# A two-part transformer kernel: token layout in the experts' stage, 512-wide scatter products, and a reordered end of three stages

## The reference

```python
for l in range(2):
    sh_m, sc_m, g_m, sh_f, sc_f, g_f = split(silu(c) @ ada_w[l] + ada_b[l], 6)
    h = rmsnorm(x, norm_mix[l]) * (1 + sc_m) + sh_m
    # three branches: differential attention, latent attention, state space (ssd)
    y = grouped_rmsnorm(ssd(...) * silu(z))          # 4 groups of 256 columns
    merged = sig(ga)*(ya@w_branch_a) + sig(gb)*(yb@w_branch_b) + sig(gc)*(y@w_branch_c)
    x = x + g_m * (merged @ w_out[l])
    h = rmsnorm(x, norm_ffn[l]) * (1 + sc_f) + sh_f
    x = x + g_f * (ffn(h @ ffn_w_up) @ ffn_w_down[l])
h = x + concat(oa, ob) @ w_out_2                      # attention of the second part
u = rms_norm(h, norm2_g)
# one group of 4, then 2 of its 8 experts per token; 32 experts of 1024 -> 512 -> 1024
y[token] += gate * (silu(u @ w_gate[e]) * (u @ w_up[e])) @ w_down[e]
out = rms_norm(h + y, final_norm_g)                   # (1, 256, 1024)
```

## Time and profile before

| | |
|---|---|
| median of 3 runs | 2047.88 us (2047.69 to 2048.53) |
| the profiled execution: its time, its span | 2048.76 us, 2047.0 us |
| busy: PE (matmul) / PEld (weight load) | 1930.3 us (94%) / 1380.8 us (67%) |
| busy: DVE (VectorE) / ACT (ScalarE) / POOL | 646.2 us (32%) / 411.3 us (20%) / 0.8 us |
| granted TensorE clock, mean | 0.967 of full speed |
| read from HBM | 439 MB, 215 GB/s over the span |

### The profile page before, as it was taken

How to read it: one execution, slowest core, us unless ns; L and a number is a source line. 1 busy time by engine, 2 the same in 40 slices (tenths; PEclk the granted TensorE clock), 3 DMA queues, 4 the chain that set the end, 5 groups by cost and what they waited for, 6 DMA issues and landing times.

```text
span 2047.0 us, 20974 instructions
## 1 busy us (share of the span) xinstructions
PE 1930.3 (94%) x8952; PEld 1380.8 (67%) x8952; DVE 646.2 (32%) x1125; ACT 411.3 (20%) x872; POOL 0.8 (0%) x9
## 2 busy tenths in 40 slices
PE   6989999889999999999989999989889999999996
PEld 3467788778888657788867888855764444545443
DVE  4442276332232434128541232034331111111111
ACT  3254121112110234312211121013311111111111
POOL 0000000000000000000000000000000000000000
PEclk9999999899999999999989999999879999999998
DMA  9733364264446563337234443353319999999960
GB/s 385 247 134 124 124 213 157 82 206 133 155 165 227 197 232 124 122 114 258 100 123 156 157 165 144 108 205 136 152 67 429 426 428 427 427 428 426 427 292 21
DMA packets 147229, 442.20 MB, mean 216 GB/s; under 512 B 8768, under 2 KB 58176, under 8 KB 133440
## 3 DMA queue, kind: packets, MB, share of 16 engines
q1 hardware_dynamic: 144704, 437.08, 56.5%
q10 hardware_dynamic: 2432, 3.78, 0.5%
HBM read 439.00 MB, written 1.84 MB: 215 GB/s over the span
## 4 chain that ended last, share of the span: by engine, by line
PE 89%; ACT 4%; DVE 4%; issue 1%; DVEq 1%; DMA 1%; PEld 0%; ACTq 0%; PEldq 0%
PE acc L705 36%; PE acc L1147 12%; PE acc L715 9%; PE aux L1164 6%; PE acc L978 4%; PE aux L978 4%; PE acc L1133 3%; PE acc L1002 3%; PE aux L628 3%; PE acc L1172 2%; PE aux L1172 1%; PE aux L644 1%; PE aux L810 1%; PE acc L1095 1%; PE aux L904 1%
## 5 line engine op out<-in xcount | busy, mean ns | idle before, releaser
L705 PE MATMUL acc<-hT,ring 128*128 128x256 f32 x2688 | 594.1, 383 | 7.1 <-ACT hT L1322 7.1
L705 PEld LDWEIGHTS acc<-hT,ring 128*128 128x128 f32 x2688 | 514.6, 192 | 82.6 <-issue 12.0
L1147 PE MATMUL acc<-ring,yT 128*64 128x512 f32 (+1 forms) x528 | 176.2, 594 | 0.0
L715 PE MATMUL acc<-ring,hT 128*128 128x512 f32 (+1 forms) x384 | 166.7, 592 | 5.8 <-ACT hT L1322 5.8
L2040 DVE SCALAR_TENSOR_TENSOR area<-acc,vectors,area 128x255 f32<-128x255 f32 (+1 forms) x176 | 72.7, 475 | 214.3 <-ACT area L1493 212.7
L715 PEld LDWEIGHTS acc<-ring,hT 128*128 128x128 f32 x384 | 73.2, 193 | 89.7 <-issue 88.0
L2273 DVE TENSOR_TENSOR xT<-xT,acc 128x1024 f32<-128x1024 f32 x17 | 20.8, 1221 | 328.8 <-PE aux L1172 328.8
L1147 PE MATMUL acc<-area,yT 128*64 128x512 f32 x384 | 112.9, 594 | 0.0
L1147 PEld LDWEIGHTS acc<-ring,yT 128*64 128x64 f32 (+1 forms) x528 | 55.5, 138 | 75.3 <-issue 75.3
L628 PE MATMUL aux<-kc,area 128*128 128x128 f32 (+1 forms) x388 | 58.9, 299 | 41.5 <-DVE area L1957 11.4
L1164 PE MATMUL aux<-ring,area 128*64 128x512 f32 (+1 forms) x272 | 95.5, 616 | 1.4 <-ACT area L1246 1.4
(11 more groups left out here) (366 smaller groups left out, 2106.3 us busy)
## 6 DMA issues: line engine op xcount, KB each, us to landing
ring<-in_w_in SPq DMA_DIRECT2D x34, 2048.0 KB, 10.2
ring<-in_ada_w SPq DMA_DIRECT2D x24, 2048.0 KB, 8.1
ring<-in_ffn_w_up SPq DMA_DIRECT2D x44, 1024.0 KB, 7.7
ring<-in_w_up SPq DMA_DIRECT2D x17, 2048.0 KB, 19.1
ring<-in_w_down SPq DMA_DIRECT2D x17, 2048.0 KB, 18.6
ring<-in_w_gate SPq DMA_DIRECT2D x16, 2048.0 KB, 15.8
area<-in_w_up SPq DMA_DIRECT2D x12, 2048.0 KB, 19.5
area<-in_w_down SPq DMA_DIRECT2D x12, 2048.0 KB, 18.1
```

The lines of the kernel that those rows point to most:

```text
L705: mm = pe.matmul(acc[LU.buf[use]][:, SEQ * j:SEQ * j + SEQ], w[:, k, c0:c0 + P], x[:, k, :], start=(k == 0), stop=(k == n - 1))
L715: mm = pe.matmul(acc[LU.buf[use]][:, at:at + width], x[:, k, P * t:P * t + P], w[:, k, :], start=(k == 0), stop=(k == n - 1))
L1147: mm = pe.matmul(dst[rows_ * e:rows_ * e + rows_, :], xg[:, b, k, rows_ * e:rows_ * e + rows_], w[:, k, :], start=(k == 0), stop=(k == KT ...
```

## The change

Three changes are merged.

1. **x by tokens in the experts' stage.** Behind the norm of the second part TensorE turns `xT` into the two accumulators (16 transposes), ScalarE copies them over `xT` as `x_tok` (2 token tiles x 1024 features). `scatter` is 4 products of 512 columns (tokens x features), stationary `pmT`, moving `ygs`, with a signal after each token tile; VectorE adds one token tile at a time. The last norm runs per token tile with ScalarE's accumulated squares, with no work on TensorE; its gain comes as a row that is loaded to all partitions (`last_gain`, one DMA more in the late loads). The stores go by halves of a token tile, two from SyncE and two from ScalarE.
2. **End of the state-space branch.** The `yo` products stand ahead of the fourth block product, the gate pieces are spread differently, and the second token tile is scaled, gated, squared, normed and turned in two halves.
3. **Norms, merge and down.** x is added, squared and summed in pairs of feature tiles (four signals, no drain ahead of them); `merged` is signalled per half, and `wo0` starts with the first four tiles; the last chunk of `ffn_w_down` runs feature tile by feature tile; the ada sums of the next layer stand behind chunks 3 and 4; `mix_gains` stands ahead of `invert_root` in the second layer.

The semaphores of the second attention are shared with those of the first (no instruction is moved).

```diff
@@ norms
-                    if k % 4 == 0:
-                        pe.wait_ge(x_sq, before + k // 4 + 1)
+                    if k % 2 == 0:
+                        pe.wait_ge(x_sq, 2 * before + k // 2 + 1)
...
-                for i in range(2):
-                    act.wait_ge(x_new, before + i + 1)
-                    act.activation(squared[:, 4 * i:4 * i + 4, :], xT[:, 4 * i:4 * i + 4, :], ACT.Square).then_inc(x_sq, 1)
+                for i in range(4):
+                    act.wait_ge(x_new, 2 * before + i + 1)
+                    act.activation(squared[:, 2 * i:2 * i + 2, :], xT[:, 2 * i:2 * i + 2, :], ACT.Square).then_inc(x_sq, 1)
@@ end of the state-space branch, TensorE
                 cb(1)
-                gate_pieces("gc0", 2, 4)
                 pe.wait_ge(st_out, l + 1)
                 decays(2)
-                gate_pieces("gc1", 0, 2)
+                gate_pieces("gc0", 2, 4)
                 diagonal(2)
                 decays(3)
-                gate_pieces("gc1", 2, 4)
-                diagonal(3)
+                gate_pieces("gc1", 0, 2)
+                pe.wait_ge(seg_ready, 4 * l + 4)
                 for g in range(SM_G):
                     mm = pe.matmul(aux[:, SEQ * g:SEQ * g + SEQ], xb[:, 12 + g, P:2 * P], stT[:, SEQ * g:SEQ * g + SEQ],
                                   start=True, stop=True)
                 mm.then_inc(yo_full, 1)
-                pe.wait_ge(y_n, 2 * l + 1)
-                pe.wait_ge(yo_out, l + 1)
+                diagonal(3)
+                gate_pieces("gc1", 2, 3)
+                pe.wait_ge(y_n, 3 * l + 1)
+                pe.wait_ge(yo_out, 2 * l + 2)
                 transposes([(y[:, 0, P * k:P * k + P], aux[:, P * k:P * k + P]) for k in range(KT)], ysT_t)
-                pe.wait_ge(y_n, 2 * l + 2)
-                pe.wait_ge(ysT_out, 3 * l + 1)
-                for k0 in (0, 4):
-                    transposes([(y[:, 1, P * k:P * k + P], aux[:, P * k:P * k + P]) for k in range(k0, k0 + 4)], ysT_t)
-                pe.wait_ge(ysT_out, 3 * l + 3)
+                pe.wait_ge(y_n, 3 * l + 2)
+                pe.wait_ge(y_out, 4 * l + 4)
+                transposes([(y[:, 1, P * k:P * k + P], aux2[:, P * k:P * k + P]) for k in range(4)], ysT_t)
+                gate_pieces("gc1", 3, 4)
+                pe.wait_ge(y_n, 3 * l + 3)
+                pe.wait_ge(ysT_out, 2 * l + 1)
+                transposes([(y[:, 1, P * k:P * k + P], aux[:, P * (k - 4):P * (k - 4) + P]) for k in range(4, 8)], ysT_t)
+                pe.wait_ge(ysT_out, 2 * l + 2)
+                pe.wait_ge(ysT_late, 2 * l + 2)
@@ the same, VectorE
+                    if hc == 3:
+                        dve.wait_ge(yo_full, l + 1)
+                        dve.wait_ge(ecs_out, l + 1)
+                        add_state(0)
                     dve.wait_ge(y_full, 4 * l + hc + 1)
                     tt(half_y, half_y, aux2, ALU.add).then_inc(y_out, 1)
...
+                D_()
+                add_state(1)
                 norm_y(0)
...
                 norm_y(1)
+                norm_y(2)
@@ merge and w_out
-                pe.wait_ge(merged, l + 1)
+                for half in range(2):
+                    pe.wait_ge(merged, 2 * l + half + 1)
+                    for j in range(4):
+                        for k in range(4 * half, 4 * half + 4):
+                            mm = pe.matmul(acc[LU.buf["wo0"]][:, SEQ * j:SEQ * j + SEQ], w[:, k, P * j:P * j + P], gates[:, 0, k, :],
+                                           start=(k == 0 and j % 2 == 0), stop=(k == KT - 1), skip_group_check=True)
+                        if half:
+                            mm.then_inc(acc_full[LU.buf["wo0"]], 1)
@@ ffn_w_down
+                    order = [(k, f) for k in range(k0, k1) for f in range(KT)] if i < 5 else [(k, f) for f in range(KT) for k in range(k0, k1)]
...
-                    if i >= 4 and l + 1 < DEPTH:
-                        ada(i - 4)
-                if l + 1 < DEPTH:
-                    ada(2)
-                    ada(3)
+                    if l + 1 < DEPTH and i in (3, 4):
+                        for n in ((0,), (1, 2, 3))[i - 3]:
+                            ada(n)
@@ second part
             sum_squares(2)
+            for t in range(T):
+                transposes([(xT[:, k, P * t:P * t + P], acc[1 - t][:, P * k:P * k + P]) for k in range(KT)], tok_t)
...
+            act.wait_ge(h_ready, 2 * KT * DEPTH + 2 * KT)
+            act.wait_ge(tok_t, T)
+            for t in range(T):
+                copy(x_tok[:, t, :], acc[1 - t]).then_inc(tok_out, 1)
@@ scatter
-                for k in range(KT):
-                    mm = pe.matmul((acc[bank], aux)[k // 4][:, SEQ * (k % 4):SEQ * (k % 4) + SEQ], ygs[:, P * k:P * k + P], pmT[:, b, :],
-                                   start=True, stop=True)
-                mm.then_inc(sc_full, 1)
+                for t in range(T):
+                    for n in range(2):
+                        mm = pe.matmul((acc[bank], aux)[t][:, 512 * n:512 * n + 512], pmT[:, b, P * t:P * t + P], ygs[:, 512 * n:512 * n + 512],
+                                       start=True, stop=True)
+                    mm.then_inc(sc_full, 1)
@@ the end
-            square_x(3)
-            root_x(3)
+            act.activation(ssq[:, 1, 0:1], epsc[:, 0:1], ACT.Sqrt)
             for t in range(T):
-                act.wait_ge(f_t, t + 1)
-                copy(fin[:, t, :], aux).then_inc(f_out, 1)
-                act.wait_ge(f_out, t + 1)
-                act.dma_start(out[0, P * t:P * t + P, :], fin[:, t, :]).then_inc(stored, 16)
+                act.wait_ge(x_last, t + 1)
+                act.activation(sqx3[:, t, :], x_tok[:, t, :], ACT.Square, accum_out=ssq[:, 0, t:t + 1])
+                act.drain()
+                root(ssq[:, 0, t:t + 1], ssq[:, 0, t:t + 1], D, (x_rt, 1))
...
+                dve.reciprocal(ssq[:, 0, t:t + 1], ssq[:, 0, t:t + 1])
+                for half in range(2):
+                    stt(fin[:, t, at:at + 512], x_tok[:, t, at:at + 512], ssq[:, 0, t:t + 1], last_gain[:, at:at + 512],
+                        ALU.mult, ALU.mult).then_inc(fin_ready, 1)
```

261 lines of the change are left out of this document (143 added, 118 removed).

## The result

The changed kernel takes **1991.26 us** (median of 4 runs, 1986.38 to 1994.47) against 2047.79 (4 runs, 2047.44 to 2048.53): ratio 0.9721, 95% interval 0.9697 to 0.9746. The four runs are two pairs: 1986.4 and 1988.3 at a mean granted clock of 0.983 and 0.982, 1994.2 and 1994.5 at 0.978; the median lies between the pairs, where no run does. The profiled execution is the fastest one: 1986.38 us, span 1984.4.

What follows compares the result with a forecast made beforehand. The prediction took TensorE's waits, its half clock and its own work as the bound (matmul 89% of the chain of waits); its terms summed to 52.7 us off the 2047.88 median, giving 1995, with a range of 1984 to 2004.

Steps and rivals of the forecast that it cites:

- end of y, two layers: End of the state-space branch: waits 2.6 instead of 8.56 us a layer, second transposes 1.07 instead of 1.97; -13.8 us.
- clock behind it: Products `bc0` and `bc1` behind y's end regain TensorE's upper clock, counted at half: -2.5 us, between 0 and -5.1.
- merge: Ahead of `wo0`: waits of 1.84 and 1.85 us go, with 1.5 us of slow products in the second layer; -5.2 us.
- end of down: End of ffn_w_down: reordered last chunk and ada sums, norm sums in 3.6 us; -2.8 and -4.8, together -7.6 us.
- second norm, turn of x: Second norm's sum ends 0.95 us earlier; the 16 added transposes stick out by 0.9 at the low clock; took -0.9 us.
- scatter: Experts' stage, 17 scatters: 512-column products take 3.45 instead of 3.65 us; 16 x 0.2, -3.2 us.
- the end: Last scatter, norm and stores: last store issued at 2027.6 instead of 2043.89; -16.3 us.
- Rival 2: Experts' stage: the loads catch up; at a 1.5% lower rate they eat the scatter's gain, 1998 us; chance 0.05.
- rival 4: Experts' stage: loads set the pace, slower; 2069 us at 15% less rate, 2076 at 358 GB/s; chance 0.01.
- rival 3: Clock stays up in more places, behind y, at three norms and in the router: 11.6 us more, 1983; chance 0.11.
- Rival 1: End of y: VectorE sets it and the clock stays low, gain per layer 4.5 instead of 6.9; 2002 us; chance 0.14.
- Rival 5: Both layers' ends: an unseen wait keeps TensorE where it was, only the program's end gains; 2031 us; chance 0.03.

Runs made afterwards that it cites:

- y_back: Changed kernel with the end of the state-space branch back in its old order, everything else kept; 2010.51 us, ratio 0.9834 to the kernel before.
- merge_back: Changed kernel with one signal for the whole merge, w_out's first chunk waiting for it with all its products; 1992.54 us, ratio 0.9739 to the kernel before.
- end_only: Kernel before with the token layout alone (turn of x, scatter, last norm and stores by tokens); 2027.68 us, ratio 0.9904 to the kernel before.
- scatter_256: Changed kernel with the scatter's products cut into pieces of 256 columns instead of 512; 1992.22 us, ratio 0.9728 to the kernel before.
- down_back: Changed kernel with ffn_w_down's last chunk and the ada sums in their old order, pairs kept; 1987.09 us, ratio 0.9732 to the kernel before.
- down_back2: Changed kernel with down's old order run once more, on another chip; 1991.73 us, ratio 0.9724 to the kernel before.
- warm: Changed kernel with 7 (the last 6) filler products of 256 columns behind the first part's four norm sums; 1981.51 us, ratio 0.9684 to the kernel before.
- warm_light: Changed kernel with the four norm waits filled by 14 (12) products of one column each; 1988.49 us, ratio 0.9723 to the kernel before.
- again: The changed kernel run once more without an edit; 1993.77 us, ratio 0.9737 to the kernel before.

## Why the prediction was right, and where it was not

1995 was forecast, 1991.26 came, inside the range. The waits were right, the sum was so in part by luck. By its own steps, against the profiled execution (span 1984.4):

| step of the prediction | forecast | measured | how |
|---|---|---|---|
| prologue | -0.4 | -0.44 | first product 39.67, now 39.23 |
| end of y, two layers | -13.8 | -13.8 | first product to `bc0`: 340.72 less 333.81 in layer 0 (6.9); in layer 1 12.6, of which 5.7 is clock ahead of it; y_back |
| clock behind it | -2.5 | -4.95 | 27.86 in both layers, from 30.05 and 30.62 |
| merge | -5.2 | -5.5 | `bc0` to `wo1` 43.22, less the line above; merge_back: 3.8 of idle time, 1.7 of slow products |
| norm behind w_out | -2.8 | -2.9 | `wo1` to up 22.48, now 21.05, twice |
| end of down | -7.6 | -7.1 | 2.6 without up's clock in layer 0, 4.5 in layer 1 |
| second norm, turn of x | -0.9 | -0.9 | without the 1.7 us of slow products at 1305; end_only |
| scatter | -3.2 | -0.2 | scatter_256 |
| the end | -16.3 | -16.9 | 27.53, now 10.65 |
| further clock | 0 | -9.9 | see below |
| sum | -52.7 | -62.6 | the spans, 2047.0 and 1984.4 |

**The step that failed is the scatter.** It divided a row of 16 instructions in a row by 16 and set it against a start-to-start time of 16 others in two groups. The difference of 0.2 us was what is left over at each half of a scatter (1.83 us instead of 1.73), which stays, and not the width. There is a slip in it besides: 8 x 7.03 / 16 is 3.52 and not 3.45, so by its own division the term was -2.2. What the runs showed in its place is 3.64 us at either width. So the pairs are 1540.68 - 1511.73 = 28.95 us apart and not 28.8.

**The step that was mis-sized is the clock**, counted at one place and at half. In the profiled execution it gave, beyond the terms above, 5.7 us in the first stretch of layer 1 (29.40 to 27.70 for the first 64 products, 11.69 to 8.86 behind `cT`, 1.2 in two smaller places), 3.06 in up of layer 0, 1.2 at router and gather, 1.66 in the loop's down, and took 1.70 back at 1305. That sums to 9.9. Not all of it differs from run to run: among ten profiles (three of the changed kernel, and scatter_256, y_back, merge_back, down_back, down_back2, warm and warm_light), 27.70 and 8.86 stand in nine, all but scatter_256, and the loop's down takes 7.13 us in all ten, against 8.79 before and 8.82 in end_only; why, no run shows. The 3.06 us of up in layer 0 came in four of the eight without fillers.

In again the kernel is 8.0 us slower, and 2048.76 - 1994.2 = 54.6 looks like the sum of 52.7. But only 2.95 of the 8.0 are a gain of this list that is gone. 1.69 are the clock's part in the end of down, where the sum fell from 5.33 to 3.62 us and now the products behind the ada sums are slow, and 3.4 are lost in the front of layer 0, where the kernel before is as quick as the changed one (the same product starts at 137.71 and 137.26 us, in again at 140.69). And the nine terms of the forecast make 52.7 as measured only because 3.0 us missing at the scatter stand against 2.45 more behind y and 0.6 more at the end. That the sum came out is luck; that the waits did is not. The largest place in the list of 9.9, in the kernel before and in the changed one, timelines of PE:

```profile
757.93 11.69 PE L715 MATMUL acc<-ring,area 128*128 128x512 f32 x24 [1.70 <-ACT area L1373]
```

```profile
737.60 8.86 PE L721 MATMUL acc<-ring,area 128*128 128x512 f32 x24 [1.70 <-ACT area L1388]
```

So the forecast's number is that of the upper group (1993.7 to 1994.7, with all waits right), and that of rival 3, 1983, is near the lower one (1985.9 to 1988.3), though not its places: it expected the norms and the router, and the router stayed at 0.50. 0.11 was too low a chance for that, since the earlier trace rows already showed one wait with slow products behind it and one without.

**Rival 1** (VectorE sets y's end) did not come: 1.42 and 0.83 us against an estimated 1.35 and 0.85. **Rival 2 and 4** (the loads): 431 GB/s in a pair's stretch, above the 358 by which rival 4 gave 2076 us, no DMA among the releasers of the experts' stage, nothing of the gain lost. **Rival 5** fell with the waits. Of the signs named ahead, those on the waits, `wo0`, the norm sums and the last store (its issue 8.2 us behind the last scatter's start, 8 forecast) came as written.

The order of down's last chunk was credited, together with the pairs, with 7.6 us. It is worth 1.9 us of waits in layer 1 and nothing in layer 0. The rest came with the pairs and the two VectorE operations that moved, 3.3 us of it because the two sums ran at the upper level (5.33 and 5.41 us before). Whether the 50.04 us behind it follow from the missing wait stays open: the profiles without it have 49.86 to 51.34 (seven) and the four with it 48.34, the kernel before and end_only among them; warm, which fills the next wait, has 48.34 without it.
